# A two-block transformer kernel on one core: the first block's dense layers in another order, with the memory's keys and values first, queries and keys turned by token, and the softmax heads beside their own projection

## The reference

```
h = rms_norm(x, g_mix)
q, k, v, z, xbc, dt = split(h @ w_in)      # 16 heads of 64; z 1024, xbc 2048, dt 16
q, k = rope(rms_norm(q, g_q)) / 8, rope(rms_norm(k, g_k))   # norm per head of 64, rope on the first 16
attn = rms_norm(softmax heads(q, k, v), g_attn)             # three dilated patterns, here one mask
ssm  = rms_norm(ssd scan(silu(conv(xbc)), softplus(dt + bias)) * silu(z), g_ssm)   # 16 heads, 4 norm groups
x = x + concat(attn, ssm) @ w_out
x = x + cross_attention(rms_norm(x, g_cross), rms_norm(mem, g_mem))   # keys and values from 256 rows of mem
x = x + square(relu(rms_norm(x, g_mlp) @ w_up)) @ w_down
```

## Time and profile before

| | |
|---|---|
| median of 3 runs | 3958.16 us (3954.49 to 3959.74) |
| the profiled execution, its span | 3960.17 us, 3958.4 us |
| mean granted TensorE clock, as a share of full | 0.923 |
| busy: TensorE, VectorE, ScalarE, GpSimd | 85%, 63%, 35%, 21% |
| TensorE starts its first matmul, ends w_out | 28.89 us, 647.7 us |

### The profile page before, as it was taken

One profiled execution on the slowest core, in us unless ns is written; L12 is line 12 of the kernel. 1 busy time (PEld: TensorE's weight loads), 2 busy tenths in 40 slices (PEclk: granted clock), 3 DMA queues, 4 the chain that ended last, 5 costly groups with the idle time before them and its releaser, 6 DMA issues.

```text
span 3958.4 us, 53297 instructions
## 1 busy us (share of the span) xinstructions
PE 3346.2 (85%) x21118; PEld 2763.2 (70%) x21118; DVE 2495.1 (63%) x3316; ACT 1382.1 (35%) x1968; POOL 837.6 (21%) x612
## 2 busy tenths in 40 slices
PE   7999888899999999899999997766666667667688
PEld 7888778899999999899998897742222223222248
DVE  5567765655455556855555665977777777555546
ACT  4346444554345443544445543221110001100124
POOL 1000001100000010000000011235665565555521
PEclk9999899999999999999999998878878888888899
DMA  6443234455555555446554355889999999999964
GB/s 207 130 126 107 91 102 149 128 182 188 185 179 184 187 190 183 138 156 187 165 166 136 121 184 164 325 330 422 421 422 422 422 421 421 421 422 421 422 264 144
DMA packets 187593, 953.17 MB, mean 241 GB/s; under 512 B 20816, under 2 KB 21072, under 8 KB 121424
## 3 DMA queue, kind: packets, MB, share of 16 engines
q0 software_dynamic: 73728, 536.90, 32.9%
q1 hardware_dynamic: 112464, 407.68, 32.8%
q10 hardware_dynamic: 1152, 5.17, 0.3%
HBM read 947.58 MB, written 2.10 MB: 240 GB/s over the span
## 4 chain that ended last, share of the span: by engine, by line
PE 62%; DMA 17%; DVE 11%; POOL 4%; ACT 3%; issue 2%; DVEq 0%; ACTq 0%; POOLq 0%; SPq 0%
PE ps L477 62%; DMA BIG<-in_peer_v,CS 7%; DMA HLF<-in_peer_v,CS 5%; DMA HF<-in_peer_v,CS 3%; DVE HL L1521 2%; POOL BIG L464 2%; POOL HLF L464 2%; DVE BIG L1525 1%; DVE BIG L2065 1%; DMA HLF<-in_peer_u,CS 1%; DMA BIG<-in_peer_u,CS 1%; DVE BIG L1521 1%; DVE TMP L1525 1%; ACT HL L1001 0%; PE ps L481 0%
## 5 line engine op out<-in xcount | busy, mean ns | idle before, releaser
L477 PE MATMUL ps<-HS,HL 128*128 128x256 f32 x11424 | 1509.1, 289 | 66.1 <-DVE HL L1521 51.6
L477 PEld LDWEIGHTS ps<-HS,HL 128*128 128x128 f32 x11424 | 1454.8, 197 | 80.6 <-DVE HL L1521 55.6
L1521 DVE TENSOR_TENSOR HL<-RAW,HL 128x1024 fp32r<-128x1024 f32 (+1 forms) x772 | 950.7, 1232 | 201.5 <-ACT HL L1001 136.3
L1001 ACT CAST HL<-RAW 128x1024 fp32r<-128x1024 f32 (+1 forms) x772 | 805.1, 1043 | 637.4 <-PE ps L477 594.8
L477 PE MATMUL ps<-BIGR,HL 128*128 128x256 f32 x6192 | 824.3, 284 | 6.5 <-DVE X L1521 5.1
L477 PEld LDWEIGHTS ps<-BIGR,HL 128*128 128x128 f32 x6192 | 783.9, 192 | 12.7 <-issue 6.7
L477 PE MATMUL ps<-BIG,HF 128*128 128x512 f32 (+1 forms) x760 | 403.1, 681 | 188.9 <-DMA BIG<-in_peer_v,CS 165.0
L477 PE MATMUL ps<-HLF,HF 128*128 128x512 f32 x656 | 344.3, 677 | 149.2 <-DMA HLF<-in_peer_v,CS 137.6
L477 PEld LDWEIGHTS ps<-BIG,HF 128*128 128x128 f32 (+1 forms) x760 | 163.2, 225 | 423.6 <-issue 389.4
L447 POOL COPY NSUM<-TMP 128x256 f32<-128x256 f32 x6 | 4.1, 686 | 2060.0 <-ACT TMP L997 2060.0
L2065 DVE CUSTOM_DVE_ANT_0 BIG<-BIG 128x2048 f32<-128x2048 f32 x133 | 305.0, 2293 | 166.9 <-DMA BIG<-in_peer_u,CS 157.7
(11 more groups left out here) (176 smaller groups left out, 2220.7 us busy)
## 6 DMA issues: line engine op xcount, KB each, us to landing
RAW<-in_w_up SPq DMA_DIRECT2D x128, 512.0 KB, 3.8
RAW<-in_w_down SPq DMA_DIRECT2D x128, 512.0 KB, 4.2
RAW<-in_w_out SPq DMA_DIRECT2D x64, 512.0 KB, 3.7
RAW<-in_w_qk SPq DMA_DIRECT2D x32, 512.0 KB, 4.5
RAW<-in_w_xbc SPq DMA_DIRECT2D x32, 512.0 KB, 3.6
RAW<-in_w_xr SPq DMA_DIRECT2D x32, 512.0 KB, 3.7
RAW<-in_w_yr SPq DMA_DIRECT2D x32, 512.0 KB, 4.1
RAW<-in_w_gr SPq DMA_DIRECT2D x32, 512.0 KB, 4.1
```

The source lines that it names most:

```text
L477: return e.matmul(o, l, r, start=start, stop=stop, skip_group_check=True)
L1001: s.done(e.copy(o, i), sig)
L1521: v.done(e.tensor_tensor(o, a, b, op), sig)
```

## The change

The layers now run as w_ck, w_cv, w_dt, w_xbc, w_v, w_qk, w_z, w_out. The diff, cut to its core (the same generators are written for TensorE, ScalarE and VectorE; one of each is shown):

```diff
-LAYERS = [("w_qk", 16, 8, 128, 2, False), ("w_v", 8, 4, 256, 4, True), ("w_dt", 1, 8, 128, 2, False),
-          ("w_z", 8, 8, 128, 2, False), ("w_xbc", 16, 8, 128, 2, False), ("w_ck", 4, 8, 128, 2, False),
-          ("w_cv", 4, 4, 256, 4, True), ("w_out", 16, 8, 128, 2, False), ("w_cq", 4, 8, 128, 2, False),
+LAYERS = [("w_ck", 4, 8, 128, 2, False), ("w_cv", 4, 4, 256, 4, True), ("w_dt", 1, 8, 128, 2, False),
+          ("w_xbc", 16, 8, 128, 2, False), ("w_v", 8, 4, 256, 4, True), ("w_qk", 16, 4, 256, 4, True),
+          ("w_z", 8, 8, 128, 2, False), ("w_out", 16, 8, 128, 2, False), ("w_cq", 4, 8, 128, 2, False),
-LATE = ("w2_ao",)
+LATE = ("w_ck", "w_out", "w2_ao")        # first three chunks: all first halves, then all second halves
# SyncE: loads in turn
+            e.dma_start(VEC[:, :], A["vecs"]).then_inc(s_vec, 16)
+            for i in range(4):
+                e.dma_start(MEM[:, 4 * i:4 * i + 4, :], A["memT"][:, 4 * i:4 * i + 4, :]).then_inc(s_mem[i], 16)
+                e.dma_start(RAW[:, i, :], STREAM[i]).then_inc(s_w[i], 16)
+            e.dma_start(CON[:, :], A["consts"]).then_inc(s_con, 16)
# ScalarE, ahead of w_ck
+            for i in range(4):
+                s.wait_ge(s_mem[i], 16)
+                for c in range(4 * i, 4 * i + 4):
+                    act(memh[0][:, c, :], MEM[:, c, :], ACT.Identity, (s_memhi, c + 1), scale=vec("g_mem", c))
+                high(i)
+                if i == 1:
+                    act(tmp(1), MEM[:, 4:8, :], ACT.Square, (s_psq, PSQ["mem"] + 1))
+            for j in range(2): ...
+                act(tmp(j), MEM[:, 8 + 4 * j:12 + 4 * j, :], ACT.Square, (s_square, SQ["mem"] + j + 1))
+            high(4)
+            high(5)
# VectorE: a group G of four query heads and four key heads, by token
+            def prepared(G):
+                total(SS, TMP[:, 0, :].rearrange("p (a d) -> p a d", d=64), ALU.add, False, (s_gsum, G + 1))
+                yield
+                v.wait_ge(s_grt, G + 1)
+                recip(SS, SS)
+                tt(xa, xa, SS.unsqueeze(2).to_broadcast([128, 16, 64]), ALU.mult)
+                for i in range(2):
+                    tt(xi, xi, vec("g_qk", 0, 128)..., ALU.mult)
+                yield
+                tt(RP[0], h[:, :, :, 0:16], CS4[:, 0, :, :]..., ALU.mult)
+                for d in (0, 8):
+                    tt(RP[1][:, :, :, d:d + 8], h[:, :, :, 8 - d:16 - d], CS4[:, 1, :, d:d + 8]..., ALU.mult)
+                tt(h[:, :, :, 0:16], RP[0], RP[1], ALU.add, (s_qkr, G + 1))
+                yield
# TensorE: its side of it, after three yields, for a in (0, 1): four transposes into PS[3]; ScalarE copies them to QK
+                    for c in range(2):
+                        for i in range(2):
+                            p = tr(PS[3][:, 256 * c + 128 * i:256 * c + 128 * i + 128], TG[G % 2][:, o:o + 128])
# all three engines
+            def norms():
+                for g in range(2):
+                    yield from ssm_norm(g)
+                while not attended[0]:
+                    yield
+                yield from rms_steps("attn", ...)
+                attended[1] = True
+                yield from until("w_z", 8)
+                for g in range(2, 4):
+                    yield from ssm_norm(g)
+            def scan_heads():
+                yield from until("w_dt", 1)
+                yield from ssd_pre()
+                yield from ssd_b()                 # after 4 chunks of w_xbc
+                yield from ssd_x(0)                # after 12
+                yield from ssd_x(4)                # after 16
+                yield from pipeline(ssd_head(h) for h in range(16))
+            def heads():
+                yield from scan_heads()
+                yield from attn_heads()            # head h starts when group h // 4 is ready
+            def inputs():
+                for G in range(4):
+                    yield from until("w_qk", 4 * G + 4)
+                    yield from prepared(G)
+                    ready[0] = G + 1
+                yield from until("w_z", 4)
+                yield from norms()
+            def mixers():
+                yield from first()                 # cuts x into HS beside w_ck and w_cv; angles; 15 steps
+                begun[0] = True
+                yield from together(heads(), inputs())
+            dense(L["w_ck"], mem, lambda c: mem_sum() if c == 0 else None, g_bg)
+            dense(L["w_cv"], mem, None, g_bg)
+            while not begun[0]:
+                next(g_bg)
+            for name in ("w_dt", "w_xbc", "w_v", "w_qk"):
+                dense(L[name], normed("g_mix"), None, g_bg)
+            dense(L["w_z"], normed("g_mix"), None, twice(g_bg))
+            while not attended[1]:
+                next(g_bg)
+            # w_out: three steps beside each of its first two units, the rest drained after the third, then head_norm("ck")
```

More of the change, by code:

```diff
@@ L171, in twice, with together @@
         step(g)
+        yield
+def together(*gens):
+    live = list(gens)
+    while live:
+        for g in list(live):
+            if next(g, g) is g:
+                live.remove(g)
         yield
@@ L661, in ssd_b @@
             def ssd_b():
-                while xbc[0] < 4:
-                    yield
+                yield from until("w_xbc", 4)
                 yield
@@ L669, in ssd_x @@
             def ssd_x(c0):
-                while xbc[0] < (17 if c0 else 12):
-                    yield
+                yield from until("w_xbc", 16 if c0 else 12)
                 yield
@@ L1225, in scalar, with attn_heads @@
-            g_nr = before()
+                yield from pipeline(ssd_head(h) for h in range(16))
+            def attn_heads():
+                live, h = [], 0
+                while h < 16 or live:
+                    if h < 16 and ready[0] > h // 4:
+                        live.append(attn(h))
+                        h += 1
+                    for g in list(live):
+                        if next(g, g) is g:
+                            live.remove(g)
+                    yield
+                attended[0] = True
@@ new lines, in heads, with inputs, mixers @@
+            def heads():
+                yield from scan_heads()
+                yield from attn_heads()
+            def inputs():
+                for G in range(4):
+                    yield from until("w_qk", 4 * G + 4)
+                    yield from prepared(G)
+                    ready[0] = G + 1
+                yield from until("w_z", 4)
+                yield from norms()
+            def mixers():
+                yield from first()
+                begun[0] = True
+                yield from together(heads(), inputs())
@@ new lines, in inputs, with mixers @@
+            def inputs():
+                for G in range(4):
+                    yield from until("w_qk", 4 * G + 4)
+                    yield from prepared(G)
+                    ready[0] = G + 1
+                yield from until("w_z", 4)
+                yield from norms()
+            def mixers():
+                yield from first()
+                begun[0] = True
+                yield from together(heads(), inputs())
+            v.wait_ge(s_vec, 16)
+            for i in range(4):
+                for c in range(4 * i, 4 * i + 4):
+                    v.wait_ge(s_memhi, c + 1)
+                    stt(memh[1][:, c, :], MEM[:, c, :], vec("g_mem", c), memh[0][:, c, :].bitcast(F32), ALU.mult, ALU.subtract,
+                        (s_memlo, c + 1))
+                low(i)
```

635 lines of the change are left out of this document (335 added, 300 removed).

## The result

The changed kernel takes 3933.51 us (median of 4 runs, 3931.39 to 3934.24), against 3958.95 for the kernel before on the same chip (4 runs, 3954.49 to 3960.38). The ratio is 0.9935, with a 95% interval from 0.9923 to 0.9947. The change is faster, by 25 us and not by the 63 that I forecast. 3933.5 lies above my range (3860 to 3928) and inside the rival "the stalls only move" (3910 to 3950).

What follows compares the result with a forecast made beforehand. TensorE was taken as the bound up to w_out's end at 647.7 us; 535 us of work plus 50 of stalls gave 585, 63 less, so 3895 us in total, range 3860 to 3928.

Steps and rivals of the forecast that it cites:

- the stalls only move: Rival: 65 to 115 us of stalls, VectorE the bound in w_xbc and w_z; 3910 to 3950 us, chance 0.19.
- the sum of 535 us: Up to w_out's end: start, units, heads, norms and other work; with 50 us of stalls, 585 us against 647.7.
- The start: Before w_ck: gains at 8.06 us, first matmul near 13.8, memory's sum done at 31.1; change -13.9 us.
- The scan beside w_v and w_qk: One scan head per unit; VectorE near 4.5 us, TensorE 4.8; +4 us of stalls.
- The series: Beside w_xbc: stall of 6.29 us, then 48 matmuls in 8.69 instead of 5.9 at half clock; 9.1 us kept.
- The table switches: ScalarE, eight loads of 1.28 us for group roots; by the skill's 1.38 us drain, some 11 us later at most.
- The groups of queries and keys: Rope by token beside w_qk: VectorE 26 us hidden under TensorE's 33; chain 10.7 us against 8.9, +4 in all.
- The norms and w_z: Beside w_z and w_out: stalls of 7.4 us for the attention's norm and 5 for each of four group norms.
- The count of steps: w_z gives 30 steps; head 15 ends near 14, attention's norm near 26, so no head is left at w_z's end.
- the rival on the slower side: Between w_z and w_out: leftover softmax heads run bare at 5.4 us each, decisive from 13 heads (71 us); chance 0.04.
- The signs: Up to w_out's end near 585 us: granted clock above 0.94, idle near 30 us, first matmul near 14.
- sign of being wrong: VectorE busy throughout w_xbc and w_v with TensorE waiting every unit, or TensorE standing between w_z and w_out.

Runs made afterwards that it cites:

- The best version: Softmax heads one step sooner, one background step per unit beside w_z, softplus series in three steps, against the changed kernel; 3897.07 us, 0.9846 of the kernel before.
- The run with half the steps: One background step per unit beside w_z instead of two, against the kernel whose heads start two steps sooner (3915.95 us); 3903.48 us.
- the spaced norms: One more unit (two steps) between sum and root of the mixers' five norms, against the changed kernel; 3931.47 us, 0.9937 of the kernel before.

## Why the prediction was wrong, point by point

**The work.** By what w_out's end shows, the sum of 535 us ahead of the stalls stands, and the stalls are the term that was mis-sized: 86 us (621.1 less 535), not 50. The stages without norms or groups came out near their terms: the end of w_cv at 74.8 us (72.1 by my terms), w_dt with w_xbc 108.0 (about 111.5). Of the 36 us between 585 and 621, w_z has 25, w_v with w_qk 7, w_out 4.5. The best version ends w_out at 583.3 us (585.62 less a wait of 2.36), so with some 48 us of stalls: 585 was reachable by this order of layers, but not by this placing of the steps.

**The start.** First matmul at 12.60 us (13.8 forecast). The memory and the gains came by 6.06, not 8.06. The sooner start brought nothing: the memory's sum ends near 31.4 us, forecast 31.1.

**The scan beside w_v and w_qk.** Charged with 4 us of stalls, it cost none. TensorE goes round in 4.84 us (237.05 to 241.89), as the 4.8 of the sum:

```profile
237.05 0.65 PE L527 MATMUL ps<-BIG 128*64 128x128 f32 x4
...
241.89 0.65 PE L527 MATMUL ps<-BIG 128*64 128x128 f32 x4
```

**The series.** 9.1 us forecast; 3.76 us of waiting and 7.51 for 48 matmuls (5.9 at full clock) make 5.4. The wait before was 6.29, and the granted clock over the 48 matmuls behind it 0.65, so they ran only in part at the 1.2 GHz that I gave them; here it was 0.77. Why the wait is shorter no run shows.

```profile
93.14 7.51 PE L527 MATMUL ps<-HS,HL 128*128 128x256 f32 x48 [3.76 <-DVE HL L1660]
```

**The table switches.** Measured at 1.28 us with the next operation 0.01 us behind (370.90 and 372.19), as in the earlier trace rows (where the gap ahead of the load is 0.07 us, not the 0.04 that I read). The drain of 1.38 us that the Trainium skill gives (ScalarE: Activation LUTs, "What ACT_TABLE_LOAD costs") doesn't show in this kernel either. Without the query and key roots' loads the kernel became no faster, though VectorE's longer chain stands against that gain.

**The groups of queries and keys: the first failed step.** "So it is hidden", I wrote, from VectorE's sum of 26 us against TensorE's 33 over eight units, and +4 us for the chain. The sum holds. The chain was under-priced even as written: 10.7 us against 8.9 is 1.8 per group, 7.2 for four. And it doesn't see the heads in it. What counts is the single step. VectorE works two units ahead of TensorE. In a step with a head's first part it has to wait for that step's scores from TensorE, so that it is level with TensorE, and then it has the two units that are already cut, 5.9 us, for all that comes before its next `low`. A maximum, exponentials, a table, roots, a reciprocal and 2.6 us of products are more than that: from the head's masked scores at 368.14 to the next `low` at 375.92 VectorE takes 7.8 us. This budget is my reading of why the step matters. The price isn't paid at the `low` itself: in this stage TensorE waits for the turned queries and keys (7.9 us) and the copied probabilities (5.6), and at a `low` only when the transposes come later. What the runs show is the placement. With 7.2 us over my terms, the scan's 4 us not used and the groups' 4 charged, the groups cost some 15 us; moving the heads by one step gave back 13.9.

**The norms and w_z: the second failed step.** I charged the stalls of w_z with 7.4 for the attention's norm and 10 for two group norms. Over its work of about 63 us by my terms (sixteen units 47, the rest of the heads 11, four sums 5) w_z has 42; over the 67.8 us for which the best version's w_z keeps TensorE busy at 0.99, 37. The trips that I had priced at 27.4 us (7.4 and four times 5) were part of it, but cost less, some 17 us in w_z and w_out together. What I had not priced was the pace. With `twice`, two steps of one chain follow each other with no unit between them, and TensorE waits out the whole way through ScalarE or VectorE: 4.23 us for a head's copied probabilities, 3.18 to 4.26 for squares. Some of it also ran at the lower clock (the unit of 4.90 us, granted 0.58). One step per unit took 18.4 us from w_z and gave 5 back in w_out.

**The count of steps.** It was used for the rival on the slower side, and there it held: nothing was left between w_z and w_out. Where it misled is that it made two steps per unit look necessary. I added the steps of heads and norms one after the other, while they advance in parallel. The run with half the steps left 5.02 + 2.35 + 2.13 = 9.5 us of bare waits.

**The signs.** The granted clock up to w_out's end was 0.95, as forecast (above 0.94), but TensorE was idle for 63 us of it, not for 30. Neither sign of being wrong that I had named came: VectorE had slack, and nothing stood between w_z and w_out.

**The chances.** "The stalls only move" had 0.19 and was right in its time (86 us of stalls against its 65 to 115), by luck, since its mechanism was wrong: VectorE is no bound in w_z (58.1 of 105.0 us busy). It is late because it waits.

**Open.** No run separates TensorE's idle time from what the lower clock costs after it; both fell together. In w_out 11.8 to 17.1 us of idle remain in every version that keeps the norms (7.7 without the five), at the last group norms and the norm of ck. No run isolates VectorE's two units of lead: the moves of the heads relieve ScalarE's queue and VectorE's at once. Not tried: the first group norms ahead of w_qk, and a deeper ring of HL buffers, which would widen the 5.9 us.

## What to carry to other kernels

Where engines with in-order queues share background work, a budget by sums per stage is not enough: ask for each step what an engine that works ahead must do between the moment when it is made level with the slowest and its next due part, and compare that with the units it has in hand. Then look at what TensorE waits for inside the steps, and not only at late weights. Spread the steps of a chain over the units: two dependent steps without work between them put the whole latency on the bound engine. More distance can also merely postpone a cost, as the spaced norms did. Count steps of chains that advance together once, and try the slower pace before calling it too slow.

## What the hardware showed that I had not expected

- VectorE's smallest operations hardly get cheaper with size: on 16 elements per partition they take 0.17 to 0.18 us and on 8 elements 0.17, so seventeen of them (3.5 us) cost as much as the wait of 3.31 us for ScalarE with its table load.
- A reciprocal is dear. For 256 elements on 128 partitions it takes 1.75 us, where a product of the same size takes 0.42 (VectorE's timeline in w_z):

```profile
459.05 0.42 DVE L1660 TENSOR_TENSOR BIG<-ps,KEEP 128x256 f32<-128x256 f32 x1 [3.82 <-PE ps L527]
...
466.20 1.75 DVE L1672 RECIPROCAL RS<-RS 128x256 f32<-128x256 f32 x1 [4.72 <-ACT RS L1084]
```
